# Gate slots given back per quarter, first gathers straight from x, held weight in another buffer

## What is computed

```
gates  = sigmoid(zg)                       # three branches, 1024 columns each
merged = gates[0]*(oa @ P_a) + gates[1]*(ob @ P_b) + gates[2]*(oc @ P_c)
x = x + merged @ w_out
x = x + HierMoE(RMSNorm(x))                # 32 experts, SwiGLU, width 256, top 2 of one group of 8
```

## Time and profile before

| what | us |
|---|---|
| median of three runs | 1017.2 |
| the profiled execution | 1017.79 |
| its span | 1015.8 |
| TensorE matmul busy | 956.4 (94%) |
| VectorE (DVE) busy | 561.1 |
| ScalarE (ACT) busy | 431.3 |
| GpSimd (POOL) busy | 58.5 |
| mean granted TensorE clock | 0.981 |

### The profile page before, as it was taken

The page is one execution under the profiler, slowest core; times in us unless marked ns, Lnnn a source line. Parts: engine busy times, 40 slices in busy tenths (PEclk is TensorE's granted clock), DMA queues, the critical chain, the costliest instruction groups (busy, mean ns, idle before and its releaser), DMA issues.

```text
span 1015.8 us, 15605 instructions
## 1 busy us (share of the span) xinstructions
PE 956.4 (94%) x5898; PEld 667.0 (66%) x5898; DVE 561.1 (55%) x1328; ACT 431.3 (42%) x920; POOL 58.5 (6%) x74
## 2 busy tenths in 40 slices
PE   9999999999999996986999999999999999977887
PEld 7888877778886441532588888777888954444323
DVE  7666787886883332221276668788868634222212
ACT  5434666666444120210353355666764441111122
POOL 1120400000010000000003004000000100000000
PEclk9999999999999998998999999999999999999989
DMA  9975644238999999999997756332599999999996
GB/s 347 352 242 193 193 138 125 84 118 328 359 385 425 404 426 423 426 427 427 418 395 242 240 178 199 125 125 67 175 356 341 407 424 407 426 422 426 426 428 278
DMA packets 99738, 313.03 MB, mean 308 GB/s; under 512 B 13488, under 2 KB 22736, under 8 KB 77648
## 3 DMA queue, kind: packets, MB, share of 16 engines
q1 hardware_dynamic: 99328, 312.04, 80.3%
q10 hardware_dynamic: 336, 0.02, 0.0%
HBM read 310.20 MB, written 1.84 MB: 307 GB/s over the span
## 4 chain that ended last, share of the span: by engine, by line
PE 77%; DMA 13%; SPq 5%; DVE 2%; issue 1%; ACT 1%; DVEq 0%; POOL 0%; POOLq 0%
PE ps L1509 16%; PE ps L1510 15%; PE ps L1511 15%; PE ps L2180 7%; DMA arena<-in_w_expert_up_dram 5%; DMA ring_rest<-in_w_expert_down_dram 5%; SPq L519 5%; PE ps L2154 3%; DMA ring_rest<-in_w_expert_up_dram 3%; PE ps L2257 3%; PE ps L1632 2%; PE ps L1534 2%; PE ps L2269 2%; PE ps L1644 2%; PE ps L2123 2%; PE ps L1660 1%
## 5 line engine op out<-in xcount | busy, mean ns | idle before, releaser
L1161 DVE TENSOR_TENSOR split_w<-arena,split_w 128x512 fp32r<-128x512 f32 (+1 forms) x352 | 233.1, 701 | 100.9 <-ACT split_w L954 97.4
L1509 PE MATMUL ps<-split_w,split_a 128*128 128x512 f32 (+1 forms) x736 | 283.8, 386 | 0.1
L1511 PE MATMUL ps<-split_w,split_a 128*128 128x512 f32 (+1 forms) x736 | 277.0, 376 | 0.0
L1510 PE MATMUL ps<-split_w,split_a 128*128 128x512 f32 (+1 forms) x736 | 276.8, 376 | 0.0
L954 ACT CAST split_w<-arena 128x1024 fp32r<-128x1024 f32 (+1 forms) x171 | 176.0, 1032 | 176.7 <-PE ps L1511 169.9
L1509 PEld LDWEIGHTS ps<-split_w,split_a 128*128 128x128 f32 x736 | 138.5, 188 | 26.9 <-issue 2.2
L1511 PEld LDWEIGHTS ps<-split_w,split_a 128*128 128x128 f32 x736 | 138.4, 188 | 25.9
L1510 PEld LDWEIGHTS ps<-split_w,split_a 128*128 128x128 f32 x736 | 138.7, 188 | 23.2
L2414 DVE SCALAR_TENSOR_TENSOR acts<-ps,wslot,acts 128x256 f32<-128x256 f32 x16 | 7.7, 484 | 167.6 <-ACT acts L2076 145.7
L2180 PE MATMUL ps<-arena,rows 128*32 128x512 f32 x416 | 91.4, 622 | 7.0 <-DMA arena<-in_w_expert_up_dram 6.2
L2180 PE MATMUL ps<-ring_rest,rows 128*32 128x512 f32 x352 | 77.3, 642 | 11.2 <-DMA arena<-in_w_expert_up_dram 11.2
(11 more groups left out here) (286 smaller groups left out, 1083.9 us busy)
## 6 DMA issues: line engine op xcount, KB each, us to landing
arena<-in_w_in_dram SPq DMA_DIRECT2D x62, 1024.0 KB, 5.2
arena<-in_w_expert_down_dram SPq DMA_DIRECT2D x34, 1024.0 KB, 21.2
arena<-in_w_expert_up_dram SPq DMA_DIRECT2D x32, 1024.0 KB, 23.5
arena<-in_w_expert_gate_dram SPq DMA_DIRECT2D x32, 1024.0 KB, 24.7
ring_rest<-in_w_expert_down_dram SPq DMA_DIRECT2D x24, 1024.0 KB, 16.9
ring_rest<-in_w_expert_gate_dram SPq DMA_DIRECT2D x22, 1024.0 KB, 23.2
ring_rest<-in_w_expert_up_dram SPq DMA_DIRECT2D x22, 1024.0 KB, 25.3
arena<-in_w_proj_a_dram SPq DMA_DIRECT2D x8, 1024.0 KB, 4.9
```

Of the source, the lines that this page charges most:

```text
L1161: dve.tensor_tensor(wlo[:, jj % 2, cols], half_slot(jj, w)[:, cols], whi[:, jj % 2, cols].bitcast(F32), ALU.subtract).then_inc(low_split i ...
L1509: pe.matmul(o, hi, rhs_hi, start=first, stop=False)
L1510: pe.matmul(o, hi, rhs_lo, start=False, stop=False)
L1511: return pe.matmul(o, lo, rhs_hi, start=False, stop=last)
```

## The change

The second branch's products get four quarters of a buffer (`gated_c`) and no longer wait; two follow split 78, two split 79, and their sums follow splits 80 and 81. SyncE gives slots 6, 2, 7, 4, 3 back one by one with finer waits on `gated`, asks for slots 14 and 15 earlier in its order, and loads the held weight in the trunk stage, once the merged rows are transposed (`mt_ready`). That weight now goes to `work`. The gathers of quads 0 and 1 read `xs` with a step of eight columns; GpSimd copies `xs` to `work` after quad 0's down product (`y_ready`), and the third gather and the first sum into `xs` wait for the copy. That sum reads `xs` itself again.

```diff
--- before.py
+++ after.py
@@ -216,6 +216,7 @@
         mixed = sb("mixed", [P, 3 * 384 + 2 * BANK + TB * A_KV * 2 * HD])
         pts = mixed[:, 0:6 * 384].rearrange("p (u c) -> p u c", u=6)
         tmp = mixed[:, 3 * 384:3 * 384 + 2 * BANK].rearrange("p (q c) -> p q c", q=2)
+        gated_c = mixed[:, 3 * 384:3 * 384 + 4 * BANK].rearrange("p (q c) -> p q c", q=4)
         k_twice = mixed[:, 3 * 384 + 2 * BANK:].rearrange("p (t h c) -> p t h c", t=TB, h=A_KV)
         mx = sb("mx", [P, 2, TB, 4])
         neg = sb("neg", [P, 2, TB, 4])
@@ -235,7 +236,7 @@
         def places(pos, n=1, routed=False):
 
             if pos == HELD and not routed:
-                return xs[:].rearrange("p t d -> p (t d)").rearrange("p (s n) -> p s n", s=1)
+                return work[:].rearrange("p t d -> p (t d)").rearrange("p (s n) -> p s n", s=1)
             if pos == 0:
                 return first_slot[:].rearrange("p (s n) -> p s n", s=1)
             s = PLACES[(pos - 2) % RING_E]
@@ -842,20 +843,27 @@
                                 load_ahead(0)
                                 sp.wait_ge(o_lo, 5)
                                 load_ahead(1, 5)
+                            if item == 40:
+                                sp.wait_ge(gated, 2)
+                                load_ahead(6)
+                            if item == 41:
+                                sp.wait_ge(gated, 3)
+                                load_ahead(2)
                             if item == 42:
-                                sp.wait_ge(gated, 4)
-                                load_ahead(2, 6)
+                                sp.wait_ge(gates_ready, 3)
+                                sp.wait_ge(gated, 6)
+                                load_ahead(7)
                             if item == 43:
-                                sp.wait_ge(gated, 8)
-                                load_ahead(4)
-                        sp.wait_ge(gates_ready, 3)
-                        load_ahead(3, 7)
+                                sp.wait_ge(gated, 7)
+                                load_ahead(4, 3)
+                        sp.wait_ge(quarter_ready, 12)
+                        load_ahead(14, 15)
                         sp.wait_ge(merged, 4)
                         load_expert(sp, l, 0, arrival(False, 0))
                         sp.wait_ge(low_split, 2 * 43)
                         load_ahead(10)
-                        sp.wait_ge(quarter_ready, 12)
-                        load_ahead(14, 15)
+                        sp.wait_ge(mt_ready, 4)
+                        load_expert(sp, l, HELD, arrival(False, HELD))
 
                         sp.wait_ge(low_split, 2 * 44)
                         load_ahead(11)
@@ -1407,11 +1415,18 @@
                             if n == 0:
                                 dve.tensor_tensor(to, pr, g, ALU.mult).then_inc(gated, 1)
                                 return
-                            dve.tensor_tensor(tmp[:, q % 2, :], pr, g, ALU.mult).then_inc(gated, 1)
-                            dve.wait_ge(gated, n * 4 + q + 1)
-                            last = dve.tensor_tensor(to, to, tmp[:, q % 2, :], ALU.add)
+                            if n == 2 and q % 2 == 0:
+                                dve.wait_ge(low_split, 82 + q // 2)
+                            product = gated_c[:, q, :] if n == 1 else tmp[:, q % 2, :]
+                            dve.tensor_tensor(product, pr, g, ALU.mult).then_inc(gated, 1)
                             if n == 2:
-                                last.then_inc(merged, 1)
+                                dve.wait_ge(gated, n * 4 + q + 1)
+                                dve.tensor_tensor(to, to, product, ALU.add).then_inc(merged, 1)
+
+                        def add_gated_c(q):
+                            dve.wait_ge(gated, 4 + q + 1)
+                            to = work[:, q % 2, q // 2 * BANK:(q // 2 + 1) * BANK]
+                            dve.tensor_tensor(to, to, gated_c[:, q, :], ALU.add)
 
                         def merged_low(i):
                             dve.wait_ge(mt_hi, i + 1)
@@ -1448,7 +1463,8 @@
 
                         for j in range(78, 82):
                             low_at(j)
-                            gate(1, j - 78)
+                            for q in (2 * (j % 2), 2 * (j % 2) + 1):
+                                gate(1, q) if j < 80 else add_gated_c(q)
                         low_at(82)
                         gate(2, 0)
                         gate(2, 1)
@@ -1885,8 +1901,8 @@
             def route_pool(pool):
 
                 half = P // 2
+                pool.wait_ge(E.y_ready, 2)
                 for nh in range(2):
-                    pool.wait_ge(x_done, 4 * nh + 2)
                     for tb in range(TB):
                         last = pool.tensor_copy(work[:, tb, :].rearrange("p (k c) -> p k c", k=KB)[:, :, nh * half:(nh + 1) * half],
                                                 quarter(xs, tb + 2 * nh).rearrange("p (c k) -> p k c", k=KB))
@@ -2098,11 +2114,17 @@
                 return 1 if n == LAST and not routed else 7
 
             def quads_pe(pe, R, a, b, routed):
+                def tokens(n, tb, k):
+
+                    if n < 2 and not routed:
+                        return xs[:, tb, :].rearrange("p (c k) -> p k c", k=KB)[:, k, :]
+                    return work[:, tb, k * P:(k + 1) * P]
+
                 def gather_pair(i):
 
                     for k in (2 * i, 2 * i + 1):
                         for tb in range(TB):
-                            mm = pe.matmul(first_gathered(k), work[:, tb, k * P:(k + 1) * P], onehot[:, 0, tb, :],
+                            mm = pe.matmul(first_gathered(k), tokens(0, tb, k), onehot[:, 0, tb, :],
                                            start=(tb == 0), stop=(tb == 1))
                         mm.then_inc(R.first_ready, 1)
 
@@ -2129,8 +2151,6 @@
 
                 def first_quad():
                     pe.wait_ge(R.onehot_ready, 1)
-                    if not routed:
-                        pe.wait_ge(x_copied, 1)
                     gather_pair(0)
                     gate_up_pair(0)
                     gather_pair(1)
@@ -2145,6 +2165,8 @@
 
                 def gather(n, ks=range(KB)):
                     pe.wait_ge(R.onehot_ready, n + 1)
+                    if n == 2 and not routed:
+                        pe.wait_ge(x_copied, 1)
                     if n == 1:
                         pe.wait_ge(R.first_act, KB - FIRST_DVE)
                     else:
@@ -2152,7 +2174,7 @@
                     for k in ks:
                         for tb in range(TB):
                             mm = pe.matmul(ps[:, 4 + k // 4, (k % 4) * QUAD:(k % 4 + 1) * QUAD],
-                                           work[:, tb, k * P:(k + 1) * P], onehot[:, n % 2, tb, :],
+                                           tokens(n, tb, k), onehot[:, n % 2, tb, :],
                                            start=(tb == 0), stop=(tb == 1))
                         if k % 4 == 3:
                             mm.then_inc(R.gath_ready, 1)
@@ -2380,21 +2402,12 @@
                                                  None, ALU.mult)
                     last.then_inc(R.gath_dve, 1)
 
-                def copied(q):
-
-                    half = P // 2
-                    nh = q // 2
-                    return work[:, q % 2, :].rearrange("p (k c) -> p c k", k=KB)[:, nh * half:(nh + 1) * half, :]
-
                 def back(n):
+                    if n == 0 and not routed:
+                        dve.wait_ge(x_copied, 1)
                     for i in range(4):
                         dve.wait_ge(R.back_ready, 4 * n + i + 1)
                         to = quarter(xs, i)
-                        if n == 0 and not routed:
-                            columns = lambda t: t.rearrange("p (c k) -> p c k", k=KB)
-                            dve.tensor_tensor(columns(to), columns(ps[:, 4 + i % 2, :]), copied(i),
-                                              ALU.add).then_inc(R.back_done, 1)
-                            continue
                         dve.tensor_tensor(to, ps[:, 4 + i % 2, :], to, ALU.add).then_inc(R.back_done, 1)
 
                 build(a)
@@ -2496,9 +2509,6 @@
                         load(sp, i + 2, False)
                 sp.wait_ge(logits_ready, TB)
                 load_second_half(sp, l, SHARED[0])
-                sp.wait_ge(squares, 2)
-                sp.wait_ge(x_copied, 1)
-                load(sp, HELD, False)
                 at = CUT * QUAD_LOADS + RING_E
                 sp.sem_inc(mid, 1)
                 quads_sp(sp, E, RING_E + 1, at, False)
```

## The result

The changed kernel takes 1031.82 us (median of 4 runs, 1031.5 to 1032.74), the kernel before, run beside it, 1017.46 (median of 4): a ratio of 1.0141 [1.0129, 1.0153], 14.4 us slower. The profiled execution took 1031.5 us.

The account below looks back on a forecast made before the run. Each layer was taken as pinned at the end of quad 1's gate and up products, TensorE before, weight transfers after. 5.1 - 0.25 = 4.9 us a layer, 9.8 for two, gave 1027.0 us; range 1015.5 to 1032.

Parts of the forecast that it names:

- 3.4 + 5: Sign before quad 1's gate and up products end: a dry spell of the transfers longer by 3.4 + 5 us.
- The pin: End of quad 1's gate and up products, about 345 us: moving it one microsecond moves the layer's end by one.
- Slots given back earlier: SyncE's earlier loads fill trunk holes, but transfers run out at about 341.5: gain 0, bounds 0 and -3.4 us a layer.
- The copies off the path: GpSimd's copies of x, moved from before the first gather, no longer slow DVE's router comparison: -0.25 us a layer.
- The late copy: GpSimd's copies after quad 0's down product, 335.4 to about 340, come well ahead of their first reader: cost 0.
- The held weight: Its 1 MB load goes out at about 287.5 instead of 312.98: no gain, cost 0, at most 1 us.
- The gathers' step: Gathers 0 and 1 read x with 32 bytes between columns: 64 loads at 80 ns more, 5.1 us a layer.
- my upper bound of 112 ns: Gathers' weight loads at DVE's stepped pace, 1.73 ns a column, would stream for 221 ns, +112 a load.
- The cover: Part of a gather's 124 ns load-and-multiply pair that could hide a slower read: 15 ns at most.
- the hidden step: Rival: TensorE reads a stepped fp32 column in the gathers as fast as a packed one; 1016.7 us, chance 0.27.
- The transfers that are not pinned: Rival: the filled 3.4 us a layer are kept past 345; 1009.9 us with a free step, chance 0.12.
- The late trunk weights: Rival: ScalarE waits for the last projection weights behind the prefetch, up to 2.5 us a layer; 1019 to 1022, chance 0.04.

Follow-up runs that it names:

- the step elsewhere: The kernel before, with the step of eight columns in the gathers of quads 2 and 5 in place of 0 and 1: 1017.8 us against 1017.72.
- the slots alone: The kernel before with gate products in four quarters and slots given back earlier, without held weight, copies or step: 1017.68 us against 1017.44, ratio 1.0001.
- the step alone: The kernel before, only its gathers of quads 0 and 1 reading the packed copy with a step of eight columns: 1032.61 us against 1017.44.
- the change without the step: The changed kernel, its gathers of quads 0 and 1 reading packed columns of x: 1016.13 us against 1017.44 for the kernel before, ratio 0.9986.
- the ladder: The kernel before, quad 1's eight gather blocks reading at steps of 1, 2, 3, 4, 5, 6, 8 and 16 columns: 1021.94 us, single execution.
- the copies on ScalarE: The kernel before with x's packed copy made by ScalarE in place of GpSimd: 1016.42 us against 1017.72, ratio 0.999.
- the halves: The kernel before, quad 1's gate products first, then up products, slots refilled after each half: 1015.47 us against 1017.72; with copies on ScalarE too, 1014.62.

## Why the prediction was right, and where its size was off

The forecast was 1027.0 and slower; measured was 1031.8, slower, 0.2 below the upper end of the range. The mechanism held, the largest term was too small. That the time still fell into the range is in part luck: the gathers' measured cost with the forecast's own 0.25 for the copies gives 1017.2 + 2 x (8.10 - 0.25) = 1032.9, outside it, and two gains that the forecast did not have, 0.42 and 0.30 us a layer (below), brought it back. The prediction's own signs say the same: loads at 335 ns where 270 to 290 were named, eight matmuls in 2.10 us for 1.7, the moment 6.96 later for some 5, the router's comparison at 0.16 as named, nothing new waiting in the trunk. The transfers lose 12 us more than before over 290 to 355 us (337 GB/s, before 414) where 3.4 + 5 were named: 5.0 of them had been fetched ahead of 290 (414 GB/s from 245 on, before 367), and 7 are the later moment. By its steps:

- **The pin.** Right, and shown from both sides. Layer 0's moment moved by 6.96 and the landing of its last down weight by 6.77 us; from the one to the other are 158.70 us before and 158.51 now. The same gathers slowed behind the moment cost nothing (the step elsewhere), and the holes filled ahead of it gained nothing (the slots alone).
- **Slots given back earlier, 0.** Right: ratio 1.0001. The place was wrong. I had one dry spell at 341.5; the changed kernel is dry in several (205 GB/s at 319, 147 at 339, 132 over 350 to 355), and with the slots alone the hole sits at 300. I had looked only at the last wait for slots. The sum did not hang on where the hole is.
- **The copies off the path, -0.25 a layer.** Sign right, size half: 0.55. The forecast counted the router's comparison alone (0.23) and gave the split beside the first pair of copies to slack on DVE. In the changed kernel splits 89 and 90 start 2.87 us apart (296.20, 299.07), and in the kernel before both stand in one block of 4.36 us without a break, and split 91 started 6.09 us behind split 89 (302.44) where it is 5.75 now (301.95). DVE had no slack there and passed 0.34 us on.
- **The late copy, 0.** Right. It runs at 340.39 for 4.25 us and nothing on the chain waits for it.
- **The held weight, 0 and at most 1.** Not separated. The changed kernel without the step is 1.3 us faster in all, of which the copies explain 1.1; what the weight adds or takes is within the rest.
- **The gathers' step, 80 ns a load, 5.1 us a layer. This is the step that failed in size.** A load measured 143 ns more, and a pair of load and multiply 126 more, where the forecast had 86 and 80. The gathers took 1.16 + 3 x 1.09 + 2 x 1.98 = 8.39 us and take 2.17 + 3 x 2.10 + 2 x 4.01 = 16.49: 8.10 a layer. Two things were wrong in the working. The 143 lie above my upper bound of 112 ns, which I took from DVE's stepped read, 1.73 ns a column; a weight load's pace at one column per 16 bytes is (335 - 83)/128 = 1.97 ns (83 from the 110 and 192 ns of 32 and 128 columns in the earlier trace rows). DVE's pace was no bound for TensorE's port. And of the rows that bounded it I chose the middle one, DVE's 86 ns. Nor did the lower row carry over: 8 bytes cost a transpose's load 58 ns, and this load 6. The cover was read rightly: the pairs went from 124 to 250 ns, 126 for a load that is 143 slower, so 17 are hidden where I had 15 at most and took 6.
- **The sum.** 8.10 for the loads, less 0.42 by which the pieces between the gathers are shorter (28.68 - 8.39 = 20.29 us, now 36.36 - 16.49 = 19.87; the same in the step alone, so it comes with the slower loads), less 0.55 of the copies: 7.1 a layer, and two layers 14.3, against 14.4 measured.

Of the rivals, the hidden step is out: 335 ns. Its argument, that 198 ns at 8 bytes is only 6 above the packed two-pass load, was a right reading of the wrong distance: at 8 bytes this load takes 196, and two columns still share 16 bytes. The transfers that are not pinned are out by the slots alone. The late trunk weights are out: the slots alone and the change without the step are not slower.

On the one place where the Trainium skill was weighed (SBUF — State Buffer, SBUF: two separate sides): the ladder agrees with its 16-byte lines and its two hits for full speed, 196 ns with two and 330 with one. It does not agree that fp32 may step up to four elements free; four elements cost the full 140 ns, and two are the most that the measurement lets pass. The measurement decides. Taken with the number of hits per line alone, that section of the Trainium skill would have said that a step of eight is slow and a step of two is not, and that is what ran.

## What to carry to other kernels

When transfers limit a stage, look for the last moment at which they were dry, and read what they waited for there: what stands ahead of it is paid in full, what stands behind it is free (here 8 us of TensorE a layer), and filling holes ahead of it without more slots moves them. A strided fp32 operand of a weight load costs next to nothing (6 ns) as long as two elements share 16 bytes, and about three quarters of the load again when each stands alone (143 on 192 ns); a layout in pairs of rows keeps it so. A slow pace of one engine is no bound for another's: where no row shows the form, the range has to reach past the nearest analogue.

## What the runs showed of the hardware

The slow pace doesn't grow with the distance: 330, 314, 318, 334 and 313 ns at steps of 16, 20, 24, 32 and 64 bytes, so 64 bytes are even a little quicker than 32 bytes. The step of 12 bytes, where some neighbours share 16 bytes and some do not, is in the middle at 261. Whole trunks shift by up to 0.6 us between profiles of kernels that are the same up to there (split 89 starts at 295.89 with the copies on ScalarE and at 296.52 with the halves beside them), so a step below a microsecond is read from an interval within one trace.
